# Moving the streamed rows of the products from 64 to 448 bytes past a multiple of 512 in a two-block transformer kernel

## The reference, cut to what matters

```
mod = c_act @ w_ada + b_ada
h = modulate(rms_norm(x, norm1_w), sh1, sc1)
p = h @ w_in                                  # q, k, v, z, decays, three gates of the short convolution
...
mix = (gate_a * (o @ w_gdn_proj) + gate_b * ((gb * conv(gc * xin)) @ w_sc_out)) @ w_o
x = x + g1 * mix
x = x + g2 * ((silu(gu[:, :2816]) * gu[:, 2816:]) @ w_ffn_out)      # gu = modulate(rms_norm(x)) @ w_ffn_in
x = modulate(rms_norm(x, normf_w), shf, scf)
...
x = x + attention(rms_norm(x) @ w_qkv) @ w_o
x = x + (silu(gate) * val) @ w_down           # gate, val = conv(rms_norm(x) @ w_up)
return rms_norm(x, final_norm)
```

## Time and profile before

| | us |
|---|---|
| runs | 936.34, 936.53, 939.70; median 936.53 |
| profiled execution, its own time | 935.56 |
| its span | 933.7 |
| TensorE busy (PE) | 889.4 |
| weight loads (PEld) | 843.7 |
| VectorE (DVE) | 673.2 |
| ScalarE (ACT) | 499.6 |
| GpSimd (POOL) | 64.0 |

### The profile page before, as it was taken

How to read it: one execution, slowest core, us unless ns; L and a number is a source line. 1 busy time by engine, 2 the same in 40 slices (tenths; PEclk the granted TensorE clock), 3 DMA queues, 4 the chain that set the end, 5 groups by cost and what they waited for, 6 DMA issues and landing times.

```text
span 933.7 us, 18526 instructions
## 1 busy us (share of the span) xinstructions
PE 889.4 (95%) x7968; PEld 843.7 (90%) x7968; DVE 673.2 (72%) x1131; ACT 499.6 (54%) x809; POOL 64.0 (7%) x86
## 2 busy tenths in 40 slices
PE   5689999899999999999999999999999999999997
PEld 2488888788899999999999999999888999999997
DVE  3877675676669989577878885668666679888653
ACT  2476764644434465545544444557556566666442
POOL 0100210111300000001000000120000200000002
PEclk9798998999999999999999999999999999999999
DMA  8743222222237986654888889544333525554631
GB/s 330 257 185 135 92 92 91 91 91 92 92 136 263 347 306 259 224 185 164 302 291 317 276 296 269 200 179 154 120 133 137 180 98 219 204 203 169 240 134 46
DMA packets 27681, 177.31 MB, mean 190 GB/s; under 512 B 2864, under 2 KB 5680, under 8 KB 7504
## 3 DMA queue, kind: packets, MB, share of 16 engines
q1 hardware_dynamic: 27600, 176.13, 53.2%
HBM read 174.29 MB, written 1.84 MB: 189 GB/s over the span
## 4 chain that ended last, share of the span: by engine, by line
PE 75%; DVE 12%; ACT 6%; DMA 4%; issue 1%; SPq 0%; DVEq 0%; ACTq 0%
PE ps L1077 41%; PE ps L1083 20%; DVE wl L1822 3%; DVE acc L1721 2%; DMA raw<-in_ada_dram 2%; PE ps L1075 2%; ACT wh L1435 1%; PE ps L1122 1%; DMA raw<-in_w_sc_dram 1%; PE ps L1130 1%; PE ps L1216 1%; PE ps L1284 1%; PE ps L1133 1%; PE ps L1081 1%; DVE KT L1704 1%
## 5 line engine op out<-in xcount | busy, mean ns | idle before, releaser
L1077 PE MATMUL ps<-HH,wh 128*128 128x256 f32 x1480 | 375.2, 289 | 3.7 <-DVE wl L1822 3.2
L1822 DVE TENSOR_TENSOR wl<-raw,wh 128x1024 fp32r<-128x1024 f32 x265 | 321.9, 1237 | 77.0 <-ACT wh L1435 76.4
L1077 PE MATMUL ps<-HH,wl 128*128 128x256 f32 x1480 | 361.4, 280 | 0.0
L1435 ACT ACTIVATE wh<-raw 128x1024 fp32r<-128x1024 f32 x265 | 272.5, 1042 | 165.6 <-PE ps L1083 109.5
L1077 PEld LDWEIGHTS ps<-HH,wh 128*128 128x128 f32 x1480 | 282.1, 191 | 13.1 <-issue 5.4
L1077 PEld LDWEIGHTS ps<-HH,wl 128*128 128x128 f32 x1480 | 281.7, 190 | 2.2 <-issue 2.2
L1083 PE MATMUL ps<-HL,wh 128*128 128x256 f32 x1480 | 228.6, 279 | 0.0
L1083 PEld LDWEIGHTS ps<-HL,wh 128*128 128x128 f32 x1480 | 197.4, 190 | 0.1
L1077 PE MATMUL ps<-FH,wl 128*128 128x256 f32 x352 | 84.5, 276 | 0.0
L1077 PE MATMUL ps<-FH,wh 128*128 128x256 f32 x352 | 84.5, 276 | 0.0
L1721 DVE SCALAR_TENSOR_TENSOR acc<-raw,silc,acc 128x512 f32<-128x512 f32 x101 | 76.7, 759 | 8.8 <-DMA raw<-in_ada_dram 5.7
(11 more groups left out here) (264 smaller groups left out, 1058.7 us busy)
## 6 DMA issues: line engine op xcount, KB each, us to landing
raw<-in_ada_dram SPq DMA_DIRECT2D x32, 1024.0 KB, 5.4
raw<-in_w_fi_dram SPq DMA_DIRECT2D x22, 1024.0 KB, 5.0
raw<-in_w_up_dram SPq DMA_DIRECT2D x22, 1024.0 KB, 4.8
raw<-in_w_rest_dram SPq DMA_DIRECT2D x20, 1024.0 KB, 4.8
raw<-in_w_in_dram SPq DMA_DIRECT2D x16, 1024.0 KB, 4.8
raw<-in_w_qkv_dram SPq DMA_DIRECT2D x12, 1024.0 KB, 4.8
raw<-in_w_o_dram SPq DMA_DIRECT2D x8, 1024.0 KB, 4.8
raw<-in_w_fo_dram SPq DMA_DIRECT2D x8, 1024.0 KB, 4.9
```

The costliest lines, as they stand in the source:

```text
L1077: e.matmul(o, w[:, k, 128 * t:128 * t + 128], x_hi[:, k0 + k, :], start=first and n + k == 0, **MM)
L1435: e.activation(whl[u % HALF][0][:, 0:n], raw[i % RAW][:, c:c + n], ACT.Copy).then_inc(*a_hi.up(u))
L1822: e.tensor_tensor(wl[:, 0:n], raw[i % RAW][:, c:c + n], wh[:, 0:n].bitcast(F32), ALU.subtract).then_inc(*v_lo.up(u))
```

## The change

The pad `home_x` shrinks from 112 to 80 floats, so that all tiles behind it begin 128 bytes lower. HH, HL, YH, YL, FH, FL, OHh, OLl, FH2 and FL2 then begin 448 bytes past a multiple of 512; R, acc, tmp and sq 352 past; cst 160 past. raw, wh, wl and X stay at 128 past.

```diff
@@ -208,7 +208,7 @@
     X = sb("X", [128, 8, T])
 
-    sb("home_x", [128, 112])
+    sb("home_x", [128, 80])
     HH = sb("HH", [128, 8, T], F32R)
```

## The result

The changed kernel took 945.48 us (median of 944.13 to 947.05), the kernel before 936.43 us in runs beside it. The ratio on record, from the executions that are compared, is 1.0125, with a 95% interval of 1.0082 to 1.0168: slower. (The two medians alone give 1.0097, inside that interval.) Executions more than 1.5% above the fastest of the same program are left out of every ratio, which takes out the profiled execution of all384up and, of the kernel before, two beside s320, s128 and d112 and two beside d112again. The profiled execution took 944.43 us with a span of 942.7 us, 9.0 us more than before.

What follows compares the result with a forecast made beforehand. TensorE's product matmuls, streaming for 95% of the span, were taken as the bound. All terms summed to 0 on 935.6 us profiled; the median 0.97 us above gave 936.5 us, own range 932 to 941, wide range 927 to 952.

Steps and rivals of the forecast that it cites:

- What bounds the kernel: Whole kernel: TensorE streams for 95% of the span, so a change in the product matmuls' start-to-start step reaches the end.
- long products: Product matmuls in the slower of two rhythms, 117.8 instead of 113.2 ns from start to start; about 1,800 of 6,264.
- Order, vector and scalar work, transfers, matmuls among moved tiles at 0: Everything but the products: queue order, DVE and ACT operations, DMA loads and small matmuls, each costed at 0.
- the 3 ns that the prediction allowed: Sign in the profile after: mean durations on DVE and ACT must stay within 3 ns, or costing them at nothing fails.
- The levels at 0: Product matmuls: the two steps, 113.2 and 117.8 ns, stay as they are; a third level would make this wrong.
- I take 0, the value of the nearest row (v2), for level and share alike: Product matmuls: neither the two steps nor the share in each rhythm changes; bounds 8.1 us less to 20.1 us more.
- v2: Products where weights and stream change places, at distance plus 64; both steps seen there, taken as evidence for 0.
- long rhythm more often: Product matmuls: more take the 117.8 ns step at the new distance; 947 us halfway, 956.6 us at most; chance 0.33.
- The other rival: Product matmuls: long rhythm not stable at the new distance, so more take the short step; limit 928.4 us; chance 0.24.
- The rule of the page TensorE: Matmul & The Clock Gate: Product matmuls: columns / 2.4 + 2.5 ns gives a floor of 109.2 ns for 256 columns, whatever an operand's place.

Runs made afterwards that it cites:

- all384up: Kernel before with 384 bytes in front of everything: streamed rows at 448, weights at 0 past, distance still minus 64; ratio 1.0000.
- s320: Kernel before with the pad home_x at 176 instead of 112 floats: streamed rows at 320, weights at 128 past, distance plus 192; ratio 0.9988.
- s128: Kernel before with the pad home_x at 128 instead of 112 floats: streamed rows at 128 past like the weights, distance 0; 956.64 us, ratio 1.0220.
- d112: Kernel before with streamed rows at 240 past, as slices 16 bytes into padded tiles, weights at 128, distance plus 112; 928.90 us, ratio 0.9957.
- d112again: The program of d112 run once more against the kernel before, for a narrower interval; 931.38 against 934.64 us, ratio 0.9959.
- experiments 1, 2, 4 and 5: Products alone over places of weights and stream (1), in finer steps (4), in long bursts (5): 113.3 to 123 ns; kernel before with places moved (2): ratios 0.9988 to 1.0147.
- the grids: Programs of product matmuls alone, not the kernel, with operands at places in steps of 64, 16 and 4 bytes; steps of 113.3 to 123 ns.
- hh448: Kernel before with only HH and HL moved to 448 past, all tiles behind them at their old place; 944.1 us, ratio 1.0121.
- w256: Kernel before with weights and X moved up 128 bytes to 256 past, streamed rows still at 64, distance plus 320; ratio 1.0147.
- rest448: Kernel before with HH and HL still at 64 past and all tiles behind home_y at 448; 939.4 us, ratio 1.0068.

## Why the prediction was wrong

**What bounds the kernel: right.** The step of a product matmul reaches the end. The count of long products read from mean durations, 1,800, came to 1,846 when counted, and it held stretch by stretch: 474 from 372 to 430 us (read as 480), 307 from 430 to 480 (307), 451 from 94 to 285 (408, a choice).

**Order, vector and scalar work, transfers, matmuls among moved tiles at 0: right.** DVE and ACT kept their busy times within 0.5 us. Their rows of more than eight operations kept their mean durations within 2 ns. A few rows of four to eight operations moved by up to 5 ns, and one of eight, wl of 512 columns, went from 920 to 878 ns. That is more than the 3 ns that the prediction allowed, but only 0.3 us in all.

**The levels at 0: right.** 113.3 and 117.8 ns are the steps before and after.

**"I take 0, the value of the nearest row (v2), for level and share alike": this failed, in the share.** Forecast 0 more long products, measured 3,641 more, 16 us by count times step, of which the granted clock gave back some 7, so that 9 us were left in the span. v2 was the right row, read wrongly. Its distance, plus 64, is the changed kernel's plus 320 less one period of 256, and there both rhythms can last; that much the row showed. I took "both occur" for "as often as now". But 192 products whose first rhythm is handed to them after a head's small matmuls say nothing on how often a start falls into each. In the changed kernel the v2 products stand at minus 64 instead, and they split as before, into 108 short and 78 long intervals. Alone, plus 320 falls into the short one in 5 of 24 starts and minus 64 in 16 of 24. And since a rhythm is kept until a wait, a transpose or a jump of the distance disturbs it, the share of starts becomes the share of time. Of the stretches of at least twelve unbroken product steps, 30 of 43 had the short step at their eleventh in the kernel before, and 69% of its intervals are short. In the changed one it was 3 of 42, and 9% are short.

**The rival "long rhythm more often" had the mechanism; that its 947 us came so near was in part luck.** It put the change halfway to a bound of 20.1 us, but 3,641 of 4,460 products turned long, 16 us of that bound, which is 952 to 953 us. The granted clock, of which the prediction had no term, gave back the rest. The measured 945.5 us lies in the prediction's wide range of 927 to 952 us and outside the forecast's own, 932 to 941. What spoke against the rival, v2, did not. The other rival, by which the long rhythm can't last at the new distance, describes plus 112 (d112), not plus 320. That the distance of the two operands sets the steps and how often each is taken is shown by experiments 1, 2, 4 and 5. What in the memory makes two reads meet, if that is what happens, and why the period is 256 bytes, was not tried and stays open.

**The rule of the page TensorE: Matmul & The Clock Gate.** The Trainium skill's 109.2 ns (section "Back-to-back issue gap") is by that section the gap of a matmul by itself, and for a stream of weight loads and matmuls in turn it says that both together set the spacing. The prediction took it as a floor for such a stream, and it was not reached at any of the 16 distances in steps of 16 bytes: the lowest lasting step was 113.3. The two independent read ports of its section "Step-by-step: what each phase is for" fit the traces in that a weight load and a stream do overlap. By the grids' 113.3 to 123 ns, the step still depends on the addresses of the two operands to each other.

**Left open.** Whether the longer steps themselves make half-clock stretches rarer. The mean granted clock of the runs was 0.990 for s128, 0.989 for hh448 and 0.989 for d112, but 0.987 for w256 and 0.985 for rest448, against 0.986 to 0.987 for before; no run tells this apart.

## What to carry to other kernels

Where float32r matmuls follow each other with a new weight load each, read the step from starts or from counts in windows and not from durations, and look whether one form has two. Then the distance between streamed rows and weights, modulo 256 bytes, is a parameter worth up to 6% of the step in places 16 bytes apart (113.3 to 120 ns) and up to 9% in places 4 bytes apart (123 ns). This was seen for loads of 128 columns and streams of 256; other sizes were not tried. Try it on a bursts-only program, with several entries per place, and prefer the distance from which every start settles in the short step over the one with the best single burst. Keep one distance for all tiles that are streamed in a row.

## What the runs showed of the hardware

- A 128x256 float32r matmul with its weight load has steps of 113.3 to about 123 ns by the distance of the two operands in SBUF, to the 4 bytes, with a period of 256 bytes.
- Two lasting steps exist at one distance (113.3 and 117.8 at minus 64 and at plus 320, which is plus 64 after one period). One is taken within a few steps of the start and kept over the 96 matmuls of a half-burst, and over the 500 of the window from 560 to 617 us in the kernel before.
- At plus 112 every one of 24 starts converges to 113.3 within about ten matmuls, at 0 every one of 24 to 120.0.
- The compared runs of the unchanged program beside d112again spanned 926.57 us (mean granted clock 0.992) to 940.06 us (0.984). The clock isn't all of it: beside rest448 it took 937.05 us at 0.992, beside d112again 929.92 us at 0.990. The redraw of the rhythms may be the rest; no trace of these runs shows it.
